# Modulation and V in two feature halves at the head of a one-core layer kernel

## The reference

```python
c_act = jax.nn.silu(c)
mod = jnp.dot(c_act, w_ada) + b_ada            # 1024 x 6144
sh_m, sc_m, g_m, sh_f, sc_f, g_f = jnp.split(mod, 6)
h = rmsnorm(x, norm_mix_g) * (1 + sc_m) + sh_m
z = h @ w_in                                   # u | v | pool | two gates
u, v = gelu(z_sgu) halves;  v = layernorm(v, v_norm_g)
s = per head, per chunk of 128 tokens: tril(sgu_w[h]) @ v + sgu_b
y_a = u * s
y_b = multiscale_pool(z_pool, pool_w) * pool_scale
merged = sigmoid(gate_a) * (y_a @ w_branch_a) + sigmoid(gate_b) * (y_b @ w_branch_b)
x = x + g_m * (merged @ w_out)
hf = rmsnorm(x, norm_ffn_g) * (1 + sc_f) + sh_f
x = x + g_f * grouped_moe(hf)                  # 16 experts, 2 per token
return rmsnorm(x, final_norm_g)
```

## Time and profile before

| | us |
|---|---|
| median of three runs | 821.66 (820.35 to 824.33) |
| the profiled execution, its own time | 820.3 |
| its span | 817.7 |
| TensorE busy | 755.9 |
| VectorE busy | 609.1 |
| ScalarE busy | 373.8 |
| GpSimd busy | 196.4 |
| DMA | 187.66 MB, mean 229 GB/s |

### The profile page before, as it was taken

One profiled execution on the slowest core, in us unless ns is written; L12 is line 12 of the kernel. 1 busy time (PEld: TensorE's weight loads), 2 busy tenths in 40 slices (PEclk: granted clock), 3 DMA queues, 4 the chain that ended last, 5 costly groups with the idle time before them and its releaser, 6 DMA issues. The chain is left out here.

```text
span 817.7 us, 10755 instructions
## 1 busy us (share of the span) xinstructions
PE 755.9 (92%) x3423; PEld 605.6 (74%) x3424; DVE 609.1 (74%) x806; ACT 373.8 (46%) x329; POOL 196.4 (24%) x74
## 2 busy tenths in 40 slices
PE   3879999999999999999999478999999999999982
PEld 1467888876787888887688467888888888888861
DVE  4972151785667565748558689999999999999976
ACT  3133352422413232323223357777777777777613
POOL 1000000500200000000043001544455555444552
PEclk9889999999999999999998579999999999999997
DMA  8979231422138192937362546599999999999652
GB/s 297 333 248 270 92 103 52 155 65 90 53 123 288 61 332 68 302 109 256 129 219 117 183 142 227 205 363 395 371 369 366 366 354 367 371 385 372 250 228 103
DMA packets 116339, 187.66 MB, mean 229 GB/s; under 512 B 6927, under 2 KB 66383, under 8 KB 115804
## 3 DMA queue, kind: packets, MB, share of 16 engines
q1 hardware_dynamic: 101660, 173.58, 60.4%
q0 software_dynamic: 4784, 7.95, 2.7%
q10 hardware_dynamic: 9872, 5.84, 2.4%
HBM read 180.47 MB, written 16.25 MB: 241 GB/s over the span
## 5 line engine op out<-in xcount | busy, mean ns | idle before, releaser
L703 DVE TENSOR_TENSOR wsplit<-raw,wsplit 128x2048 fp32r<-128x2048 f32 x132 | 299.5, 2291 | 89.9 <-ACT wsplit L494 64.3
L640 ACT ACTIVATE wsplit<-raw 128x2048 fp32r<-128x2048 f32 x96 | 184.0, 1920 | 74.1 <-PE ps L1256 74.1
L442 POOL DMA_INDIRECT expert_rows<-work,dest_now x15 | 108.2, 7212 | 114.3 <-DVE work L1160 114.3
L1254 PE MATMUL ps<-wsplit,hgT 128*128 128x512 f32 x272 | 110.0, 405 | 5.0 <-DVE hgT L1079 5.0
L1256 PE MATMUL ps<-wsplit,hgT 128*128 128x512 f32 x272 | 107.6, 396 | 0.0
L1255 PE MATMUL ps<-wsplit,hgT 128*128 128x512 f32 x272 | 106.6, 392 | 0.0
L1254 PE MATMUL ps<-hT,wsplit 128*128 128x512 f32 x256 | 102.4, 400 | 1.2 <-DVE mx L833 1.0
L1255 PE MATMUL ps<-hT,wsplit 128*128 128x512 f32 x256 | 101.0, 395 | 0.0
L1256 PE MATMUL ps<-hT,wsplit 128*128 128x512 f32 x256 | 101.0, 395 | 0.0
L755 DVE SCALAR_TENSOR_TENSOR raw<-raw,c_silu 128x256 f32 (+1 forms) x128 | 62.0, 484 | 17.7 <-DMA raw<-in_w_ada 13.7
L1254 PEld LDWEIGHTS ps<-wsplit,hgT 128*128 128x128 f32 x272 | 51.9, 191 | 15.5 <-DVE hgT L1079 5.6
(11 more groups left out here) (240 smaller groups left out, 1224.5 us busy)
## 6 DMA issues: line engine op xcount, KB each, us to landing
raw<-in_w_exp_gate SPq DMA_DIRECT2D x32, 1024.0 KB
raw<-in_w_exp_up SPq DMA_DIRECT2D x32, 1024.0 KB
raw<-in_w_exp_down SPq DMA_DIRECT2D x32, 1024.0 KB
raw<-in_w_ada SPq DMA_DIRECT2D x24, 1024.0 KB
raw<-in_w_in SPq DMA_DIRECT2D x20, 1024.0 KB
expert_rows<-zeros ACTq DMA_DIRECT2D x4, 1024.0 KB, 9.1
raw<-in_w_branch_a SPq DMA_DIRECT2D x4, 1024.0 KB
raw<-in_w_branch_b SPq DMA_DIRECT2D x4, 1024.0 KB
```

The lines of the kernel that those rows point to most:

```text
L442: g.indirect_dma_start(out=y_dram, out_offset=bass.IndirectOffsetOnAxis(ap=dest_now[:, 0:1], axis=0), in_=y, in_offset=None, bounds_check= ...
L640: A_(wsplit[:, c, 0, :], raw[:, c, :], ACT.Copy).then_inc(hi_ready, 1)
L703: V.tensor_tensor(wsplit[:, n, 1, :], raw[:, slot, :], wsplit[:, n, 0, :].bitcast(F32), ALU.subtract).then_inc(lo_ready, 1)
L1254: nc.tensor.matmul(out, w_hi, m_hi_, start=first, stop=False)
```

## The change

- **Tokens first.** SP issues the four token tiles before any of w_ada.
- **w_ada by halves.** The same 8 MB come in eight pieces of 512 columns by half of the features: scale and shift of features 0 to 511 (pieces 0 to 3), then of 512 to 1023 (pieces 4 to 7). VectorE forms all of them (`ada_head`): four steps of 128x512, each waiting for the one before. TensorE's row products and ScalarE's row copies are gone. `mod_columns` is called twice, with 8 instructions each.
- **h by halves.** ScalarE scales the tokens; TensorE transposes all four token tiles, feature tiles 0 to 3 into banks 4 to 7, tiles 4 to 7 into banks 0 to 3, whence ScalarE saves them to SBUF (`xT_late`). ScalarE does the affine step and the high part, VectorE the low part.
- **V's order.** Chunk n now has output half n % 2, feature half n // 2. TensorE does chunk 0, tokens 0 to 255 of chunk 1, the second column products, chunk 2, the other tokens of chunk 1, chunk 3. Chunks 0 and 1 need only features 0 to 511.
- **Zero rows** are issued by SP behind V's last chunk, from a zeroed `wsT` in pieces of 1024 columns instead of 128; sgu_w is loaded behind them. Its transposes stand on TensorE behind the first u chunk, the copy and the load of sgu_b on ScalarE one chunk later.

The diff, cut to its core:

```diff
+ADA_PLACE = (0, 1, 2, 3, 5, 6, 8, 9)
+V_PLACE = (4, 7, 10, 11)
+V_SPLIT = (0, 2, 1, 3)
...
-        zeros = sb("zeros", [P, P])
...
-        ada_prod = raw[:, 4, :].rearrange("p (k n) -> p k n", k=ND)
-        macc_a = work[:, 0:RAW_ADA // 2 * CC]
-        mod_row = work[0:1, 2 * D:2 * D + CC]
+        macc_a = raw[:, 4, :].rearrange("p (b n) -> p b n", n=512)
+        xT_late = raw[:, 5, :].rearrange("p (k n) -> p k n", n=SEQ)
...
+            if n < U0:
+                return V_SPLIT[n]
...
-                    sp.dma_start(wnat.rearrange("p (h j) -> p h j", h=NH),
-                                 A["sgu_w"][0].rearrange("h i j -> i h j")).then_inc(wnat_in, 16)
...
-                if n < RING_A:
-                    first_used(RING_A + n)
+            for t in range(NT):
+                sp.dma_start(x_tiles[:, t, :], x_rows[:, t, :]).then_inc(x_in[t], 16)
+
...
+                c0 = D * (1 - block % 2) + 512 * (block // 2)
+                load(ADA_PLACE[i] % RING_A, w_ada[:, 4 * kh:4 * kh + 4, c0:c0 + 512], 4)
+
+            def load_v(n):
+
+                half, kh = n % 2, n // 2
+                load(V_PLACE[n] % RING_A, w_in[:, 4 * kh:4 * kh + 4, D + half * 512:D + half * 512 + 512], 4)
+
+            for i in range(4):
+                load_ada(i)
+            sp.wait_ge(ada_used, 1)
+            load_v(0)
+            sp.wait_ge(ada_used, 2)
+            load_ada(4)
+            sp.wait_ge(ada_used, 3)
+            load_ada(5)
+            sp.wait_ge(ada_used, 4)
+            load_v(1)
+            sp.wait_ge(lo_ready, 1)
+            load_ada(6)
+            sp.wait_ge(ada_used, 5)
+            load_ada(7)
+            sp.wait_ge(ada_used, 6)
+            load_v(2)
+            sp.wait_ge(lo_ready, 2)
+            load_v(3)
...
+            for t in range(NT):
+                sp.dma_start(y_pairs[t].rearrange("p (a n) -> p a n", n=D),
+                             wsT.unsqueeze(1).broadcast_to([P, 2, D])).then_inc(y_zero, 16)
+            sp.dma_start(wnat.rearrange("p (h j) -> p h j", h=NH),
+                         A["sgu_w"][0].rearrange("h i j -> i h j")).then_inc(wnat_in, 16)
...
+            for n in range(U0, G0):
+                if n < U0 + 2:
+                    sp.wait_ge(ada_used, n - U0 + 7)
...
-            g.memset(zeros[:, :], 0.0).then_inc(zero_row, 1)
+            g.memset(wsT, 0.0).then_inc(zero_row, 1)
...
-                    act.wait_ge(ws_t, 1)
-                    A_(wsT, ps[:, 5:7, :].rearrange("p b n -> p (b n)"), ACT.Copy).then_inc(ws_ready, 1)
-
-            for k in range(ND):
+            act.wait_ge(rms_ready, 1)
+            for t in range(NT):
+                A_(x_tiles[:, t, :], x_tiles[:, t, :], ACT.Copy, scale=stats[:, t:t + 1]).then_inc(xhat_ready, 1)
+            act.wait_ge(xT_t, NT)
+            for b in range(2):
+                A_(xT_late[:, 2 * b:2 * b + 2, :], ps[:, 2 * b:2 * b + 2, :], ACT.Copy).then_inc(xT_saved, 1)
+            hi(split_slot(0), *raw_place(0))
+
...
+                act.wait_ge(gain_ready, k // 4 + 1)
+                x_k = ps[:, 4 + k, :] if k < 4 else xT_late[:, k - 4, :]
+                A_(x_k, x_k, ACT.Identity, scale=gain[:, k:k + 1], bias=mod_cols[:, k:k + 1]).then_inc(h_aff, 1)
...
                 act.wait_ge(h_aff, k + 1)
...
+                A_(hT[:, 0, k, :], x_k, ACT.Copy).then_inc(h_hi, 1)
...
+            h_half(0)
+            hi(split_slot(1), *raw_place(1))
+            hi(split_slot(2), *raw_place(2))
+            h_half(4)
+            hi(split_slot(3), *raw_place(3))
...
-            act.wait_ge(zero_row, 1)
-            for t in range(NT):
-                act.dma_start(y_pairs[t].rearrange("p (a n) -> p a n", n=P),
-                              zeros[:, :].unsqueeze(1).broadcast_to([P, 2 * D // P, P])).then_inc(y_zero, 16)
...
+                if n == U0 + 1:
+
+                    act.wait_ge(ws_t, 1)
+                    act.wait_ge(y_zero, 16 * NT)
+                    A_(wsT, ps[:, 6:8, :].rearrange("p b n -> p (b n)"), ACT.Copy).then_inc(ws_ready, 1)
+                    act.wait_ge(ws_ready, 1)
+                    act.dma_start(bsb, A["sgu_b"][0].rearrange("h i -> (h i)").partition_broadcast(P)).then_inc(bsb_in, 16)
...
-            for i in range(RAW_ADA // 2):
...
+            dve.wait_ge(squares, NT)
+            inv_rms(0, NT)
+            V.tensor_copy(fin_rms[:, :], stats[:, 0:1]).then_inc(rms_ready, 1)
+
...
+                r, block = ADA_PLACE[i], i // 2
+                acc = macc_a[:, block, :]
                 dve.wait_ge(landed[r % RING_A], 16 * (r // RING_A + 1))
-                step(V.tensor_tensor(ada_prod, raw[:, r % RING_A, :].rearrange("p (k n) -> p k n", k=ND),
-                                     c_silu[:, :].unsqueeze(2).broadcast_to([P, ND, CC]), ALU.mult))
+                if i % 2:
+                    dve.wait_ge(ada_used, i)
+                for k in range(4):
+                    w_k, c_k = raw[:, r % RING_A, k * 512:(k + 1) * 512], c_silu[:, 4 * (i % 2) + k:4 * (i % 2) + k + 1]
+                    if k == 0 and i % 2 == 0:
+                        ins = V.tensor_scalar(acc, w_k, c_k, None, ALU.mult)
+                    else:
+                        ins = V.scalar_tensor_tensor(out=acc, in0=w_k, scalar=c_k, in1=acc, op0=ALU.mult, op1=ALU.add)
+                    if k < 3:
+                        step(ins)
+                        done()
+                    else:
+                        ins.then_inc(ada_used, 1)
+
...
+                dve.wait_ge(mod_mm, h + 1)
+                step(V.tensor_tensor(mod_cols[:, c8], ps[:, bank, 0:4], cols[:, 40 + 4 * h:44 + 4 * h], ALU.add))
+                step(V.tensor_tensor(mod_cols[:, c], ps[:, bank, 4:8], cols[:, 32 + 4 * h:36 + 4 * h], ALU.add))
...
+                V.scalar_tensor_tensor(out=gain[:, c], in0=mod_cols[:, c8], scalar=1.0, in1=cols[:, c8],
+                                       op0=ALU.add, op1=ALU.mult).then_inc(gain_ready, 1)
...
+            dve.wait_ge(c_ready, 1)
+            for i in range(4):
+                ada_head(i)
...
+            modulation(0, 0)
+            lo_n(0, raw_place(0)[0])
+            for k in range(4):
+                h_low(k)
+            ada_head(4)
+            ada_head(5)
+            lo_n(1, raw_place(1)[0])
+            ada_head(6)
+            ada_head(7)
+            modulation(1, 7)
+            lo_n(2, raw_place(2)[0])
+            for k in range(4, ND):
+                h_low(k)
+            lo_n(3, raw_place(3)[0])
...
+            def mod_columns(h, bank):
+
+                pe.wait_ge(ada_used, 4 * h + 4)
+                for b in range(2):
+                    for m in range(4):
+                        mm = nc.tensor.matmul(ps[:, bank, 4 * b + m:4 * b + m + 1],
+                                              macc_a[:, 2 * h + b, m * P:(m + 1) * P], ones[:, 0:1],
+                                              start=True, stop=True)
+                mm.then_inc(mod_mm, 1)
...
+            pe.wait_ge(cols_ready, 1)
+            for t in range(NT):
+                pe.wait_ge(xhat_ready, t + 1)
                 for k in range(ND):
...
+                    mm = nc.tensor.transpose(ps[:, (k + 4) % ND, t * P:(t + 1) * P], x_tiles[:, t, k * P:(k + 1) * P],
...
+            pe.wait_ge(xT_saved, 1)
+            mod_columns(0, 0)
...
+                        if half == 0 and t == 0:
+                            pe.wait_ge(h_lo, kk + 1)
...
+            pe.wait_ge(gain_ready, 1)
+            pe.wait_ge(xT_saved, 2)
+            v_chunk(0, range(NT), True)
+            v_chunk(1, range(2), False)
+            mod_columns(1, 7)
+            v_chunk(2, range(NT), True)
+            v_chunk(1, range(2, NT), True)
+            v_chunk(3, range(NT), True)
...
+                if n == U0 + 3:
+                    pe.wait_ge(ws_ready, 1)
                 by_feature(n % 2, hT, 2 * (n - U0))
+                if n == U0:
+                    pe.wait_ge(causal, 1)
+                    pe.wait_ge(v_gelu, 2 * NT)
+                    for h in range(NH):
+                        mm = nc.tensor.transpose(ps[:, 6 + h // 4, (h % 4) * P:(h % 4 + 1) * P],
+                                                 wnat[:, h * P:(h + 1) * P], ident[:, :])
+                    mm.then_inc(ws_t, 1)
```

More of the change, by code:

```diff
@@ L293, in _, with load_ada @@
-            for n in range(V0, G0):
-                if n < RING_A:
-                    first_used(RING_A + n)
+            for t in range(NT):
+                sp.dma_start(x_tiles[:, t, :], x_rows[:, t, :]).then_inc(x_in[t], 16)
+            def load_ada(i):
+                block, kh = i // 2, i % 2
+                c0 = D * (1 - block % 2) + 512 * (block // 2)
[3 more added lines that the diff above has]
+                load(V_PLACE[n] % RING_A, w_in[:, 4 * kh:4 * kh + 4, D + half * 512:D + half * 512 + 512], 4)
@@ L296, in _ @@
                 else:
                     sp.wait_ge(lo_ready, n - RING_A + 1)
[L298 to L301, removed]
+                if n < P0:
```

(57 more changed lines are left out.)

105 lines of the change are left out of this document (25 added, 80 removed).

## The result

The changed kernel takes 812.49 us (median, 810.42 to 813.29) against 822.38 before; the ratio is 0.9883, with an interval of 0.9864 to 0.9902. That is 9.9 us faster where 5.5 were forecast, and 812.49 lies inside the range. Its profiled execution took 810.42 us, its span 808.6, 9.1 under the span before.

The account below looks back on a forecast made before the run. TensorE, busy 92% of the span, was taken as the bound, its head waiting for bytes V's first half does not need. 6.5 us earlier less 0.95 gave 5.5 saved, forecast 816.2 us, range 811.5 to 820.2.

Parts of the forecast that it names:

- the hole: TensorE's wait between the second column products and chunk 2 of V: 3.7 us, from 56.3 to 60.0.
- the 88 to 91: Sign that the prediction is right: the first u chunk starts at 88 to 91 us.
- the forecast's own bounds: Whole kernel's time, allowing for slow stretch, columns, landings and operation length, without the rivals: 813.5 to 818.5 us.
- the rival in which the clock stays up: TensorE, head columns and V: no second slow stretch, columns at full speed; 9.5 us saved, 812.2; chance 0.15.
- the sum: Whole kernel: u chunks 6.5 us earlier, less 0.95 for the moved sgu_w transposes, so 5.5 us saved.
- I keep 14.0: V's chunk 0 on TensorE takes 14.0 us as before, since it starts at the low clock, against 11.1 at full clock.
- the row at 493.49: Eight products in the earlier trace, 3.41 us instead of 1.84, pricing a restart at the low clock at 1.6 us.
- VectorE's split of chunk 2 (2.25): Before V's second half: VectorE does this split ahead of h's lows, 2.25 of TensorE's wait of 3.7 us.
- The clock's fall behind the hole: TensorE at chunk 2 of V: the clock drops to 0.50 after the wait, costing 2.0 us.
- VectorE did not become the bound: Rival in head and V: 128x512 operations from SBUF cost 1.04; 1.7 us saved, 820.0; chance 0.13.
- The gain was not given back later: Rival after V: gain lost at a stage whose wait does not depend on TensorE; 821.7 us; chance 0.07.
- The queue did not hold the loads: Rival at the first u chunk: zero rows hold SP's load queue; 10.5 us slower, 832.2; chance 0.05.

Follow-up runs that it names:

- Halves undone: Changed kernel with the second column products moved ahead of V's first chunk, so V waits for both halves of the modulation: 825.11 us, ratio 1.0051.
- cover: Changed kernel with one token tile of chunk 1 (tokens 256 to 383) moved in front of chunk 2: 807.39 us, ratio 0.9838.
- zero_act: Changed kernel with the zero rows issued by ScalarE again, in pieces of 128 columns, behind the router loads: 810.74 us, ratio 0.9863.
- split_early: Changed kernel with VectorE's split of chunk 2 in front of the second modulation instead of behind it: 812.16 us, ratio 0.9887.
- warm: Changed kernel with 16 token transposes repeated on TensorE ahead of the first column products: 810.8 us, ratio 0.9874.
- best: Changed kernel with both remaining token tiles of chunk 1 between second column products and chunk 2, plus split_pair's order: 806.19 us, ratio 0.9814.
- split_pair: Changed kernel with VectorE's splits of chunks 0 and 2 ahead of their modulation and ScalarE's first high part ahead of its second affine step: 812.41 us, ratio 0.9876.
- best_warm: The kernel of best with the 16 repeated token transposes ahead of the first column products: 804.63 us, ratio 0.9786.
- before_zero_sp: Kernel before, with only the four zero-row issues moved from ScalarE's queue to SP's, ahead of the first u chunk: 817.88 us, ratio 0.9962.
- before_x_first: Kernel before, with only the four token loads moved ahead of all of w_ada: 824.51 us, ratio 1.0038.

## Why the prediction was right, and where it was off

**The mechanism held.** In the profiled execution V started at 33.94 (forecast 34.8); the hole was 3.4 (3.7), before chunk 2, with the clock at 0.50 behind it; there was no hole at chunk 3; the u chunks started at 86.60 (forecast 89.7, outside the 88 to 91 that I had named); the load queue had time to spare. Halves undone confirms the cause, cover the price of the hole.

**That the time fell inside the range was in part luck.** 812.49 lies below the forecast's own bounds, 813.5 to 818.5. The range reached down to 811.5 only to take in the rival in which the clock stays up (812.2). That rival gives nearly the measured time, and it did not happen: the clock was at 0.50 in the head's columns and behind the hole.

**The size was off, most by one term.** At the spatial product the gain in the profiled execution was 8.7 us, against 5.5 in the sum. The 3.2 are: V's start 0.9 (the columns begin 0.2 earlier, take 3.55 instead of 4.0, and V follows 3.4 behind them instead of 3.6); chunk 0 with half of chunk 1 took 18.3 (33.94 to 52.20) instead of 19.6, 1.3; the hole 0.3; V behind it 29.15 instead of 29.7, 0.55; columns and transposes 0.1. Of the 4.4 us between the 9.9 measured and the 5.5, that leaves 1.2: the 0.4 on the way to the router, and 0.8 by which the profiled execution's own time shrank more than its span. No run explains either.

So the step that failed most is "I keep 14.0": I carried over chunk 0's own slow stretch, 5.7 us long in the trace of before. Counted from V's first product to the clock's return it lasts 3.0 in the changed kernel, 2.9 in cover, 3.2 in zero_act and 4.4 in split_early, whose code is the same up to there; 3.8 in warm, 3.5 in best, 5.5 in split_pair, 5.6 in best_warm; and with the head of before, 5.7, 4.0 (before_zero_sp) and 4.9 (before_x_first). It is a value that varies with the execution, and I had one sample of it; the row at 493.49, whose eight products I used to price the hole, was another, 3.2. With 3.0 in place of 5.7 the forecast would have had 1.3 more.

**The hole's cause was named wrongly, its size rightly.** The prediction put VectorE's split of chunk 2 (2.25) on the path. It lay beside ScalarE's three steps, which end at the same time; split_early moved it away and won nothing. I had checked ScalarE against VectorE in the head, but not here, and I had priced its affine step like a high part, at 0.5; two of them with the high part took 2.05 (54.54 to 56.59), not 1.5. In the head too the two end together (low part at 33.10, ScalarE's high part at 32.95).

**The clock's fall behind the hole held.** The row at 57 to 61 us shows 0.57 behind the hole, at a price of 1.65 us (29.15 for what takes 27.5 at full clock), forecast 2.0. It varies too: from chunk 2's first product to the clock's return there are 3.4 us here, 3.5 in zero_act, 4.1 in warm, 4.4 in split_early and 5.4 in split_pair. The Trainium skill (TensorE: Matmul & The Clock Gate, the section on HAM oscillation) warns of gaps between bursts that let the clock fall back; the trace agrees, and so do the runs with the hole covered, cover and best, at 1.00 in the same stretch.

**The rivals.** The clock stayed up in neither of the two places that the first rival names. VectorE did not become the bound: 128x512 from SBUF costs 0.79. The gain was not given back later. The queue did not hold the loads, though a zero row took 12.4 us to land in the median and sgu_w 16.4, more than the 9.1 and 11.0 with which I had priced that rival: they overlap.

## What to carry to other kernels

When a head is bound by bytes that only part of the next stage needs, order loads, formation and products by that part, and count what stands in the hole between the parts. Keep some full products that need nothing new for that hole: here one token tile in it gave back 3.7 us by the trace, and two tiles with split_pair's order 5.6, since they saved the length and the slow clock. Parts of such a change may each be worthless or worse alone (tokens first cost 3 us in the kernel before), so take the chain that ends last from the new order, and list all engines' chains to that point before blaming one. Look past the total, too: here a rival that did not happen had the better number.

## What was unexpected of the hardware

TensorE's clock fell at 26.7 us, 5.1 us after its last transposes, in the changed kernel, but at 24.7 in split_early, 2.3 us after them, with the same code up to there. In warm, with sixteen transposes at 24.30 and the columns up to 29.4, it stayed at 1.00 until 29.8. The slow stretch behind a restart lasted 2.9 to 4.4 us for the same code (cover, split_early), and up to 5.6 with other orders of the same products: 1.4 us of run time between its ends.

The clock that the view gives ahead of the first change it shows is not to be relied on. In the changed kernel it prints 1.00 from the start, but the token transposes start 0.21 us apart until 20 us and 0.11 apart behind it, so the clock was at its lower level until then, and rose while TensorE did nothing but transposes.
